# Expert layers: 32 tokens of a dense tile are served by gathered rows, the other 352 stay dense, and the pair search looks at 65 sums in place of 256

## The reference, cut to what matters

```
s = einsum('thcd,hcnd->thcn', q, keys)            # q = x @ w_q
sv, si = top_k(s, 16)
cand = (sv[:, :, 0, :, None] + sv[:, :, 1, None, :]).reshape(n, 8, 256)
best, bi = top_k(cand, 16)
eidx = i1 * 128 + i2;  gate = softmax(best)
act = gelu(einsum('td,ted->te', x, u_tab[eidx])) * gate
out = einsum('te,ted->td', act, v_tab[eidx])
```

## Time and profile before

| what | us |
|---|---|
| median of 3 runs | 4435.25 (4434.05 to 4435.57) |
| span of the profiled execution, first to last instruction | 4431.5 |
| PE busy, DVE busy | 4200.0, 2900.3 |
| ACT busy, POOL busy | 731.9, 1585.0 |
| dots L555, both layers | 1357.7 |
| sums L592, both layers | 1357.3 |

### The profile page before, as it was taken

The page is one execution under the profiler, slowest core; times in us unless marked ns, Lnnn a source line. Parts: engine busy times, 40 slices in busy tenths (PEclk is TensorE's granted clock), DMA queues, the critical chain, the costliest instruction groups (busy, mean ns, idle before and its releaser), DMA issues. The chain is left out here.

```text
span 4431.5 us, 46041 instructions
## 1 busy us (share of the span) xinstructions
PE 4200.0 (95%) x16590; PEld 2488.8 (56%) x16590; DVE 2900.3 (65%) x5840; ACT 731.9 (17%) x1492; POOL 1585.0 (36%) x1462
## 2 busy tenths in 40 slices
PE   7986889999999999999989998999999999999998
PEld 3643647676544555545447875576755455554553
DVE  6747627999876665556543147599997676664763
ACT  4122410163000000000013122104700000000000
POOL 0002200075675555545200000003766665554640
PEclk9997999999999999999989999999999999999999
DMA  4213731268999999989711104013899999997993
GB/s 181 80 45 129 268 129 48 77 178 275 357 409 362 387 362 358 361 310 382 293 43 66 67 10 124 24 53 125 236 362 359 363 410 364 363 358 284 410 358 115
DMA packets 354895, 1050.79 MB, mean 237 GB/s; under 512 B 31785, under 2 KB 132617, under 8 KB 343226
## 3 DMA queue, kind: packets, MB, share of 16 engines
q0 software_dynamic: 148096, 545.34, 32.2%
q1 hardware_dynamic: 107392, 452.36, 27.3%
q10 hardware_dynamic: 99196, 50.34, 4.0%
HBM read 991.16 MB, written 56.76 MB: 236 GB/s over the span
## 5 line engine op out<-in xcount | busy, mean ns | idle before, releaser
L592 PE MATMUL banks<-blocks,picked_T 128*128 128x512 f32 x3072 | 1357.3, 594 | 16.0 <-DVE picked_T L772 16.0
L555 PE MATMUL banks<-h_dense_T,blocks 128*128 128x384 f32 x4096 | 1357.7, 487 | 0.0
L555 PEld LDWEIGHTS banks<-h_dense_T,blocks 128*128 128x128 f32 x4096 | 779.2, 191 | 579.5 <-issue 98.3
L592 PEld LDWEIGHTS banks<-blocks,picked_T 128*128 128x128 f32 x3072 | 587.0, 191 | 708.7 <-issue 654.9
L383 POOL DMA_INDIRECT expert_rows<-in_pk_u_dram,expert x512 | 665.9, 1300 | 480.1 <-DVE own_dots L787 254.8
L383 POOL DMA_INDIRECT expert_rows<-in_pk_v_dram,expert x512 | 605.1, 1182 | 508.6 <-DVE acc L806 257.1
L806 DVE SCALAR_TENSOR_TENSOR acc<-expert_rows,expert_weight,acc 128x1024 f32<-128x1024 f32 x504 | 623.8, 1283 | 80.9 <-DMA expert_rows<-in_pk_v_dram,expert 79.6
L787 DVE CUSTOM_DVE_ANT_0 expert_rows<-expert_rows,h_rows 128x1024 f32<-128x1024 f32 x512 | 601.8, 1222 | 54.4 <-DMA expert_rows<-in_pk_u_dram,expert 53.2
L772 DVE TENSOR_TENSOR picked_T<-dense_act,shared 128x384 f32<-128x384 f32 x246 | 210.2, 855 | 555.3 <-PE banks L592 547.3
L408 ACT ACTIVATE dense_act<-banks 128x384 f32<-128x384 f32 x246 | 120.6, 490 | 2228.1 <-PE banks L555 2218.1
L374 POOL TENSOR_SCALAR expert_rows<-iota,picked_T 128x128 f32<-128x128 f32 x384 | 251.1, 672 | 472.7 <-ACT picked_T L414 415.0
(11 more groups left out here) (504 smaller groups left out, 3681.0 us busy)
## 6 DMA issues: line engine op xcount, KB each, us to landing
blocks<-in_pk_u_turned_dram SPq DMA_DIRECT2D x256, 512.0 KB, 6.7
blocks<-in_pk_v_dram SPq DMA_DIRECT2D x256, 512.0 KB, 6.7
gates_dram<-shared ACTq DMA_DIRECT2D x48, 1024.0 KB, 5.3
shared<-gates_dram SPq DMA_DIRECT2D x32, 1536.0 KB, 10.9
ada_block<-in_ada_rest_dram SPq DMA_DIRECT2D x32, 1280.0 KB, 7.5
blocks<-in_pk_w_q_dram SPq DMA_DIRECT2D x32, 512.0 KB, 3.6
MIXT<-in_ev_w_in_dram SPq DMA_DIRECT2D x16, 512.0 KB
expert_rows<-in_pk_u_dram,expert POOLq DMA_INDIRECT x512, 8.8
```

The source lines that it names most:

```text
L555: mm = pe.matmul(dense_dots(c), u[:, k * P:(k + 1) * P], HT[:, k, :], start=(k == 0), stop=(k == KD - 1))
L592: mm = pe.matmul(ps[:, at_:at_ + HALF], wt[:, c % WEIGHED, z * P:(z + 1) * P], v[:, half_ * HALF:(half_ + 1) * HALF], start=(c == 0), stop ...
```

## The change: what it does

Of the third dense tile (now tile 2) the last 32 tokens leave the dense way: `DENSE` is 352. For these 32 tokens the 128 slots are dealt out over the 128 partitions, four copies of 32 tokens with 32 slots each, so 32 gathered rows of U and 32 of V serve them ("unit 0"). SP copies the 32 normalised tokens four times into a third row of `H` before the layer. The order of the gathers is now U of unit 0, U of the first row tile, V of unit 0, V of the first tile, U and V of the second: 576 rows, 36 in 7 chunks, from chunk 0 on. The four partial sums of unit 0 are added by four matmuls with a stacked identity (`fold_rows`), once per layer, in chunk 39.

The dots and the weighing are 352 wide; the spread does 88 groups of four tokens in place of 96. The 96 dense tokens of the split tile are summed as 64 + 32 tokens: the 64 as two matmuls, which write the two halves of the 1024 values to PSUM partitions 0 to 63 and 64 to 127 of bank 4, the 32 as four matmuls onto four groups of 32 partitions of bank 5. They come before the two whole tiles in a chunk. At the end DVE adds the split tile in seven pieces.

The pair search keeps, of the 256 pairs, four blocks of 16, 16, 16 and 18 (65 are looked at), which hold all pairs that can be among the 16 best; the place in a block is turned back into the two ranks by a few shifts.

```
-DENSE_TILES = (2, 3, 4)
+DENSE_TILES = (3, 4, 2)
-DENSE = ND * P
+OWN = 32
+WAYS = P // OWN
+DENSE = ND * P - OWN
+SPLIT_PARTS = ((0, 64, 4), (64, 32, 5)) if OWN == 32 else ((0, 64, 4),)
-GAPS = (8, 17, 26, 35, 44)
+GAPS = (7, 15, 23, 31, 39)
-BEFORE = 33
-FIRST_ROWS = 3
+BEFORE = 40
+BLOCKS_OF_PAIRS = tuple((16 * k, 2 ** k - 1, 2 ** k + (k == 3), 16 >> k) for k in range(4))
+PAIRS_KEPT = 65
+UNIT_STEPS = (OWN_STEPS, SLOTS, SLOTS)
+PHASES = (("u", 0), ("u", 1), ("v", 0), ("v", 1), ("u", 2), ("v", 2))
-    return 8 if c < FIRST_ROWS else 3
+SIDE_STEPS = 5
-    return min(2 * SLOTS * NR, 4 * n + 2 * n // 3)
+    return min(ROWS, 36 * (c + 1) // 7)
+            pool.wait_ge(spread, DENSE)
+            for phase in PHASES:
...
-                    mm = pe.matmul(dense_dots(c), u[:, k * P:(k + 1) * P], HT[:, k, :],
+                    mm = pe.matmul(dense_dots(c), u[:, k * P:(k + 1) * P], HT[:, k, 0:DENSE],
...
+                for first, size, bank in SPLIT_PARTS:
+                    at_, width = bank * HALF, D * size // P
+                    token = WHOLE * P + first
+                    for q in range(P // size):
+                        here = part_of(first, size, q)
+                        mm = pe.matmul(ps[here:here + size, at_:at_ + width],
+                                       wt[:, c % WEIGHED, token:token + size],
+                                       v[:, q * width:(q + 1) * width],
+                                       start=(c == 0), stop=(c == P - 1))
-                for z in range(ND):
+                for z in range(WHOLE):
...
+            def fold_rows():
+                pe.wait_ge(own_sum, 1)
+                pe.wait_ge(dots_out, dots_with(FOLD_AT)[0] - 1)
+                for q in range(WAYS):
+                    mm = pe.matmul(ps[q * OWN:(q + 1) * OWN, fold_bank:fold_bank + OWN_WIDTH], fold[:],
+                                   folded[:, q * OWN_WIDTH:(q + 1) * OWN_WIDTH], start=True,
+                                   stop=True)
...
-                        line.count(search(step, cand[:, z, :], cand[:, 4 + z, :], best_of[:, z, h, :],
-                                          at_of[:, z, h, :]))
+                        line.count(search(step, cand[:, z, 0:PAIRS_KEPT], cand[:, 4 + z, 0:PAIRS_KEPT],
+                                          best_of[:, z, h, :], at_of[:, z, h, :]))
...
+            def add_split():
+                dve.wait_ge(sum_done, 1)
+                dve.wait_ge(fold_out, 1)
+                line.count(dve.tensor_tensor(acc[P - OWN:P, 0, :], folded[P - OWN:P, :],
+                                             g_row[P - OWN:P, 1, :], ALU.mult))
+                for first, size, bank in SPLIT_PARTS:
+                    width = D * size // P
+                    for q in range(P // size):
+                        here = part_of(first, size, q)
+                        line.count(dve.tensor_tensor(
+                            acc[first:first + size, 0, q * width:(q + 1) * width],
+                            ps[here:here + size, bank * HALF:bank * HALF + width],
+                            g_row[first:first + size, 1, q * width:(q + 1) * width], ALU.mult))
...
+            sp.wait_ge(h_ready, ND)
+            for q in range(WAYS):
+                sp.dma_start(H[q * OWN:(q + 1) * OWN, NR, :], h_of(ND - 1)[P - OWN:P, :]
+                             ).then_inc(first_blocks, 16)
```

More of the change, by code:

```diff
@@ L367, in _ @@
                 pool.wait_ge(cols_out, z + 1)
-                for t in range(P):
+                for t in range(min(P, DENSE - z * P)):
                     n = z * P + t
@@ L568, in spread_tile @@
             def spread_tile(z):
-                for g in range(z * P // 4, (z + 1) * P // 4):
+                for g in range(z * P // 4, min((z + 1) * P, DENSE) // 4):
                     if g % 2 == 0 and g >= 6:
@@ L667, in by_head_dense @@
             def by_head_dense(h):
[L669 removed]
+                for at_, a, many, few in BLOCKS_OF_PAIRS:
+                    shape = [P, ND, many, few]
                     line.count(dve.tensor_tensor(
[L671 to L672 removed]
+                        cand[:, 0:ND, at_:at_ + many * few].rearrange("p z (a b) -> p z a b", a=many),
+                        top[:, 0:ND, 2 * h, a:a + many].unsqueeze(3).to_broadcast(shape),
+                        top[:, 0:ND, 2 * h + 1, 0:few].unsqueeze(2).to_broadcast(shape), ALU.add))
                 for step in range(4):
@@ L778, in add_to_x, with own_v @@
+            def own_v(u):
+                first = first_row(("v", u))
+                own = slice(UNIT_AT[u], UNIT_AT[u] + UNIT_STEPS[u])
+                dve.wait_ge(own_gelu, u + 1)
+                line.then(dve.tensor_tensor(act_w[:, own], act_w[:, own],
+                                            picked[:, ND + u - 1, 2, :] if u else own_gate[:],
                                             ALU.mult))
-                line.then(dve.tensor_tensor(X[:, t, :], X[:, t, :], acc[:, 0, :], ALU.add))
@@ L847, in normalize @@
                 dve.tensor_tensor(h, h, shift[:, g, :], ALU.add).then_inc(h_ready, 1)
+            ins = dve.tensor_tensor(fold[:], ident[:, 0:OWN], ident[:, OWN:2 * OWN], ALU.add)
+            for q in range(2, WAYS):
+                line.then(ins)
+                ins = dve.tensor_tensor(fold[:], fold[:], ident[:, q * OWN:(q + 1) * OWN], ALU.add)
+            line.then(ins)
             for c in range(CODES):
@@ L858, in _ @@
             last = (x for i in range(ND, NT) for x in by_head(i))
-            taken = (x for n in range(NR) for x in own_rows(n))
+            taken = (x for kind, u in PHASES for x in (own_u if kind == "u" else own_v)(u))
             for _ in range(BEFORE):
@@ L863, in _ @@
                 weigh(c)
-                for _ in range(side_steps(c)):
+                for _ in range(SIDE_STEPS):
                     next(last, None)
```

280 lines of the change are left out of this document (178 added, 102 removed).

## The result

The changed kernel takes 4412.8 us (median of four runs) against 4434.7 beside it on the same chip: ratio 0.9941, interval 0.9929 to 0.9953. It is faster, by 22 us and not by the 117 of the forecast; the time lies above the range. The profiled spans are 4412.7 and 4431.5.

What follows compares the result with a forecast made beforehand. PE, busy 95% of the span, was taken as the bound, with transfers late next. PE's path -80.8 us and stops +23 gave -57.8 per layer, -116 for two: 4318 us from a profiled span of 4431.5; range 4248 to 4400.

Steps and rivals of the forecast that it cites:

- (b): PE's sums per chunk: split third tile 1.56 us against 1.72, three turns at 0.09 included; -20.4 us per layer.
- (e): PE's stops in the loop: 34 us per layer in place of 11, +23; bounds 9 and 60.
- (a): PE's dots, 352 columns for 384: 4.73 us per chunk against 5.16, all 128 chunks; -55.0 us per layer.
- R2: Rival: the two 64-wide halves of the split tile run one after the other; +27 us per layer, 4489; chance 0.11.
- (c): The spread: 88 groups of four tokens in place of 96; -8.4 us per layer.
- (d): After the last sums: DVE adds the split tile in seven pieces, 4.3 us against 1.22; +3 us per layer.
- transfers: Part of the loop's stops: 430 MB at 410 GB/s take 1048 us against PE's 1046; 2 us per layer.
- pause: Part of the loop's stops: gathers pausing at the one remaining turn from U to V rows; 22 us per layer.
- it begins when the gates land, 14.2 us after the spread: DVE's start in the first chunks: 42.4 us at the least against 38.3; 4 us of stop.
- R4: Rival: the forecast with dearer turns (0.17 each, +31 us per layer) or 395 GB/s; 4350 to 4400; chance 0.12.
- R1: Rival: transfers don't bind in the loop, the lead covers the pauses; -83 us per layer, 4269; chance 0.20.
- R3: Rival: transfers bind far lower, at 358 GB/s; a layer some 70 us slower, 4580; chance 0.02.

Runs made afterwards that it cites:

- run 3: Changed kernel, two variants: without the split tile's four 32-wide matmuls, 4355.7 us; with its 96 tokens summed as one 96-wide piece, 4399.6 us.
- run 8: Kernel before the change with only the search over 65 pairs and its index steps: 4431.4 us against 4437.6, ratio 0.9990.
- Run 4: Changed kernel with GpSimd starting its gathers only when the first two groups of gates have landed: 4391.5 us against 4413.
- run 5: Changed kernel with no rows in the first two chunks, then 37/7 a chunk in place of 36/7: 4388.8 us against 4413.
- run 2: Changed kernel with every second gather left out from the eleventh row on: 4357.0 us, ratio 0.9825 to the kernel before.
- the last run: Changed kernel with gathers behind first gates, length-dealt rows starting two chunks later and ending at chunk 115, row-dots gelu two chunks earlier, 96-wide piece: 4305.4 us.
- run 1: Changed kernel with gathers from the eleventh row on bringing 64 of 128 partitions: 4609.5 us, ratio 1.038 to the kernel before.

## Why the prediction was wrong

Its sign and most of its mechanism were right; two terms of the sum were mis-sized, (b) by 28 us per layer and (e) by 19.

(a) Dots: 4.733 per chunk against 4.73 forecast. Right; 6.9 of it is seen in the early dots alone.

(b) Sums: the step that failed most. The halves do run beside each other (R2 is out: the 64-wide part fits in 1.01). The price of a turn was taken as 0.09, though the working itself gave 0.08 to 0.2 from the earlier trace rows, and no reason was given for the low end. A chunk without dots takes 5.209, where 3.43 of whole tiles and 1.29 of split pieces are 4.72: three turns cost 0.49, not 0.27. Of the starts: 0.09 from dots to the 64-wide records, 0.15 in that part beyond its 0.86, 0.14 in the 32-wide part beyond its 0.43, and 0.11 at the first whole record, after which the next starts 534 ns later and not 429. So (b) is +0.06 per chunk, +7.6 per layer, in place of -20.4; the parts of run 3 confirm it, with one turn less (0.139 beyond the work) and with none (0.06 less in all). Read per visit, with its entry and its exit, the same row gives the price: 3.63 + 1.01 from start to start, for 3.43 + 0.86 to 0.93 of work, is 0.28 to 0.35 for two turns, so 0.42 to 0.52 for three. The Trainium skill, TensorEngine Tiling (Array Packing), Key Properties, says that changing the tiling mode drains TensorE. The estimate that the prediction set beside it, 0.50 for three turns and +9 per layer, was the better one, and these runs agree with it.

(c) The spread gave 7.3 and 6.5 (beside its five chunks of dots) for 8.4. (d) The end cost 1.3 and 3.1 for 3. The search, put at nothing, goes with 2.8 and 0.7 off the query stage (2.8 and 2.2 in run 8). "No gap" was read from the earlier trace rows, which begin at 830; from 669 to 830, in the queries, PE did wait 2.0 us for DVE in layer 0. (The "-24" there is 120 x 0.2, the searches ahead of the loop; the 80 in the loop would be 16.)

(e) Stops: 52.6 in layer 0 (10.7 before the loop, 41.9 in it) in place of 34. The transfers were sized well: in chunks 20 to 25, at the turn and at 111 there were 31.7 us for the 24 of "transfers" and "pause" and some slow records; 433 MB at 392 GB/s until 2160 for 430 at 410, and three of the places named (chunks 24, 88 and 112) are where stops lay. What failed is the line "it begins when the gates land, 14.2 us after the spread": the first weighing came 28.9 after it (27.6 in layer 1), and DVE's start cost 20.4 (10.7, then 9.7) and not 4. The rest of that line was right: DVE's work to the end of the third weighing is 28.7 for the 28 to 30 forecast, and with 28.9 in place of 14.2 the same working gives 28.9 + 28.7 - 38.3 = 19. The prediction noted that rows would now stand there (before, the first stood in chunk 3) and counted them as DVE's work alone, not as transfers that meet the gates. Run 4 shows that the gathers made the gates late, run 5 what DVE's rows cost there.

With the 4.4 us that arose ahead of both layers this makes the sum: -115.6, +56 for (b), +37.2 for (e), +3 for the spread, -3.5 for the searches, -1.6 for the ends, +4.4: -20, against -18.8 in the spans.

R4 had the price of a turn right, 0.17 against 0.163 measured (0.49 for three); its 4350 to 4400 was too low because it kept the 4 us for DVE's start. R1 and R3 are out: transfers bind (run 2), at 402 to 411 GB/s. The Trainium skill, DMA: Bandwidth & Descriptors, Where 436 GB/s comes from, has about 358 GB/s per core as the bound from HBM. The 402 GB/s over 1101 us of the last run speak against it, and the measurement decides.

## What to carry to other kernels

Price a change of TensorE's tiling per visit, entry and exit, by leaving the split out: work saved inside a visit of a few matmuls can be less than its turns, as 0.43 against 0.49 here. When work is dealt to steps of a loop, deal it by each step's length and not by their number, and leave the first steps free for the engine that must get ahead. When a buffer or an index becomes ready earlier, ask which transfer its loads will now meet.

## What was not expected of the hardware

A gather into 64 partitions moved its packets at 224 ns in place of 146, and slowed whole 512 KB blocks beside it from 158 to 254 ns a packet (run 1). The Trainium skill, Advanced Engine Details and Errata, DMA Bandwidth Details, says that SBUF has 16 ports that each serve 8 partitions. By an estimate from that, a transfer into half of the partitions reaches half of the ports and gets half of the rate; 236 GB/s against 410 agrees with it in direction. No run here gathered into other halves, so the cause is not shown.
